# A two-part network on one core: filler matmuls dealt out anew, small tables written by GpSimd, gating tables requested one stage earlier

## The reference

```python
# first model: 16 meta tokens + 256 tokens, width 1024
h = h + 0.5 * swiglu(rms_norm(h, g_ffn1), w1_gate, w1_up, w1_down)
h = h + hybrid_mixer(rms_norm(h, g_mix), ...)      # the attention part, below
h = h + 0.5 * swiglu(rms_norm(h, g_ffn2), w2_gate, w2_up, w2_down)

def hybrid_mixer(u, ...):
    c_q, c_kv, k_pe, fox_qkv, f_logit = split(u @ w_in)
    q = rope(rms_norm(rms_norm(c_q) @ w_uq))           # 8 heads of 96
    k, v = ... rms_norm(c_kv) @ w_ukv ...              # 64 + 32 for keys, 64 for values
    o_mla = causal_attention(q, k, v)
    fq, fk, fv = ... fox_qkv ...                       # 8 more heads of 64
    cum = cumsum(log_sigmoid(f_logit + b_forget))      # adds cum[t] - cum[s] to the scores
    o_fox = causal_attention(rms_norm(fq), rms_norm(fk), fv, cum)
    return concat(o_mla, o_fox) @ w_out

# second model, first layer: the same gated mixer on the latent rows (from the first model)
# and on the 256 context rows (which depend on nothing of the first model)
def gmlp_mixer(h, w_in, b_in, ln_g, ln_b, w_s, b_s, w_out, b_out):
    u, v = split(gelu(h @ w_in + b_in))                # 2048 columns each
    v = layernorm(v, ln_g, ln_b)
    v = einsum('gpq,bcqgd->bcpgd', w_s, v) + b_s.T     # mixes 128 positions
    return (u * v) @ w_out + b_out
# then a routed mixture of experts, a recurrent second layer, a second mixture, a norm
```

## Time and profile before

| | |
|---|---|
| median of 3 runs (lowest, highest) | 3248.51 us (3243.59, 3256.89) |
| the profiled execution's own time / its span | 3252.2 us / 3250.5 us |
| PE busy | 2752.6 us (85% of the span) |
| DVE, ACT, POOL busy | 1076.6 (33%), 521.1 (16%), 319.7 us (10%) |
| mean granted clock of TensorE | 0.938 of full speed |
| the part from the first fox norm to the end of attention | 369.9 to 676 us |
| the latent rows' v stage to the end of `gm_u` | 981.2 to 1107.2 us |

### The profile page before, as it was taken

One profiled execution on the slowest core, in us unless ns is written; L12 is line 12 of the kernel. 1 busy time (PEld: TensorE's weight loads), 2 busy tenths in 40 slices (PEclk: granted clock), 3 DMA queues, 4 the chain that ended last, 5 costly groups with the idle time before them and its releaser, 6 DMA issues. The chain is left out here.

```text
span 3250.5 us, 59101 instructions
## 1 busy us (share of the span) xinstructions
PE 2752.6 (85%) x25857; PEld 1987.0 (61%) x25857; DVE 1076.6 (33%) x2222; ACT 521.1 (16%) x1141; POOL 319.7 (10%) x356
## 2 busy tenths in 40 slices
PE   8999898989998996878777399798989976977775
PEld 7886665668876785444444144388878964444443
DVE  3562326425651413110000421366555522100002
ACT  1001122320001101000000200154444411000001
POOL 1000000000000000201110200132322201111110
PEclk9999989989999997999999699799999987999998
DMA  7684332136865306999999421000000019999994
GB/s 261 236 253 141 106 107 78 40 110 233 256 202 168 104 26 255 338 402 396 405 402 404 137 78 36 19 4 3 4 3 3 4 53 372 403 406 407 407 405 190
DMA packets 297238, 638.61 MB, mean 196 GB/s; under 512 B 29252, under 2 KB 198423, under 8 KB 262436
## 3 DMA queue, kind: packets, MB, share of 16 engines
q1 hardware_dynamic: 254896, 558.44, 46.9%
q10 hardware_dynamic: 30500, 61.96, 5.3%
q0 software_dynamic: 11600, 14.59, 1.4%
HBM read 634.79 MB, written 21.08 MB: 202 GB/s over the span
## 5 line engine op out<-in xcount | busy, mean ns | idle before, releaser
L2426 PE MATMUL bank<-expert_weights,ex_xt 128*64 128x256 f32 x2688 | 314.0, 389 | 90.3 <-DMA expert_weights<-in_moe_w_up_dram 78.0
L2426 PEld LDWEIGHTS bank<-expert_weights,ex_xt 128*64 128x64 f32 x2688 | 216.0, 140 | 202.9 <-issue 133.0
L533 PE MATMUL bank<-u,weights 128*128 128x272 f32 (+1 forms) x1408 | 318.7, 390 | 12.0 <-DVEq L556 12.0
L533 PEld LDWEIGHTS bank<-u,weights 128*128 128x128 f32 x1408 | 270.7, 192 | 59.8 <-DVEq L556 12.6
L1334 DVE SCALAR_TENSOR_TENSOR ada_acc<-ada_w,cond,ada_acc 128x512 f32 (+1 forms) x336 | 227.6, 747 | 1.6 <-PEq L505 1.6
L2337 DVE TENSOR_TENSOR ex_hidden<-ex_silu,bank 128x256 f32<-128x256 f32 x64 | 27.0, 421 | 596.5 <-ACT ex_silu L2475 596.5
L610 PE MATMUL bank<-rw_mixed,weights 128*128 128x512 f32 (+2 forms) x448 | 189.1, 583 | 31.7 <-DVEq L623 28.2
L2426 PE MATMUL bank<-weights,ex_xt 128*64 128x256 f32 x1408 | 168.7, 396 | 38.3 <-DMA weights<-in_moe_w_up_dram 37.0
L2447 PE MATMUL bank<-expert_weights,ex_hidden_turned 128*64 128x512 f32 x672 | 159.3, 617 | 21.7 <-DVE ex_hidden_turned L2340 21.7
L2426 PEld LDWEIGHTS bank<-weights,ex_xt 128*64 128x64 f32 x1408 | 113.5, 143 | 99.9 <-issue 63.5
L610 PEld LDWEIGHTS bank<-rw_mixed,weights 128*128 128x128 f32 (+1 forms) x448 | 84.1, 189 | 137.1 <-issue 135.2
(11 more groups left out here) (593 smaller groups left out, 4264.7 us busy)
## 6 DMA issues: line engine op xcount, KB each, us to landing
expert_weights<-in_moe_w_gate_dram SPq DMA_DIRECT2D x84, 1024.0 KB, 24.3
expert_weights<-in_moe_w_up_dram SPq DMA_DIRECT2D x84, 1024.0 KB, 24.6
expert_weights<-in_moe_w_down_dram SPq DMA_DIRECT2D x84, 1024.0 KB, 24.5
ada_w<-in_ada_w_dram ACTq DMA_DIRECT2D x24, 2048.0 KB, 9.2
weights<-in_moe_w_gate_dram SPq DMA_DIRECT2D x44, 1024.0 KB, 24.2
weights<-in_moe_w_up_dram SPq DMA_DIRECT2D x44, 1024.0 KB, 24.3
weights<-in_moe_w_down_dram SPq DMA_DIRECT2D x44, 1024.0 KB, 24.6
weights<-in_ga_w_in_dram SPq DMA_DIRECT2D x32, 1024.0 KB, 5.6
```

What stands on the lines that cost most here:

```text
L533: last = nc.tensor.matmul(k.bank[b + side * NB][:, 0:N], w[:, f, c * P:(c + 1) * P], rhs[:, f, 0:N], start=(f == 5), stop=(f == 4))
L2426: last = nc.tensor.matmul(half_cols(k.bank[2 + side], t), xt[:, s, f * SLOTS:(f + 1) * SLOTS], w[:, q * 512 + t * 256:q * 512 + t * 256 + ...
```

## The change

- The v pieces are dealt out anew: three units in each of `fqn` and `fkn` (16 pieces behind the loop in place of 8), two in `cq` and `ckv` as before, and six in `expand_stage` in place of eight (none in its last two heads). The banks, the take-over by DVE (`keep_v`, one more in `fqn` and `fkn`, two fewer in `expand`), the GELU shares and SP's requests follow. In `expand_stage` PE issues its first 8 pieces before it waits for `w_uq` and `w_ukv`.
- `mla_sums_of` is written by POOL in `expand_stage`, one stage earlier. The gate tables are preset by POOL in `row_norm_stage`; DVE's two presets in `rope_stage` are gone.
- In attention the u pieces stand behind `scores(u)` and ahead of `turn(u-2)`; they are dealt 2, 1, 1, 2, 1, 1 and, from turn 30 on, 2, 2, 1, 1, 2. ACT takes units over in turns 5, 11, ... 35.
- The four gating tables are requested on ACT at the start of `gmlp_v_stage`, behind the bias; the block that held the requests is gone.

```diff
@@ head_norm_stage (fqn, fkn)
-        block.sync(ahead.feed_v)
+        block.sync(lambda sp: ahead.feed_v(sp, 3))
-            ahead.v_pieces(pe, 2 * DC - 2 * heads)
+            ahead.v_pieces(pe, 3 * DC - 2 * heads)
             ahead.keep_v(dve)
+            ahead.keep_v(dve)
@@ row_norm_stage, pool
-            pool.memset(of[:, :, :], 0.0).then_inc(zeroed, 1)
...
+            for g in gates:
+                pool.memset(g, 1.0).then_inc(preset, 1)
@@ row_norm_stage, tensor
-            pe.wait_ge(marked, HEADS)
@@ expand_stage, tensor
-            k.stream.wait(pe, seg, 0, 0)
-            k.stream.wait(pe, seg, 0, 1)
...
             for h in range(HEADS):
-                ahead.v_pieces(pe, DC)
                 if h < 6:
+                    ahead.v_pieces(pe, DC)
+                    if h == 0:
+                        k.stream.wait(pe, seg, 0, 0)
+                        k.stream.wait(pe, seg, 0, 1)
                     values(h)
@@ expand_stage, pool
+            pool.memset(sums_of[:, :, :], 0.0).then_inc(zeroed, 1)
...
+                pool.memset(sums_of[:, h, h:h + 1], 1.0).then_inc(marked, 1)
@@ rope_stage, vector
-            link(nc.vector.memset(gates_q[0:2, :, :], 1.0))
-            link(nc.vector.memset(gates_k[0:2, :, :], 1.0))
@@ attention_stage, tensor
                     scores(u)
+                ahead.u_pieces(pe, (2, 1, 1, 2, 1, 1)[u % 6] if u < 30 else (2, 2, 1, 1, 2)[u - 30])
...
-                if u < 30:
-                    ahead.u_pieces(pe, (2, 2, 1, 2, 1)[u % 5])
@@ attention_stage, scalar
-                if u % 5 == 0 and 5 <= u <= 30:
+                if u % 6 == 5:
                     ahead.keep_u_scalar(act)
@@ gmlp_v_stage, scalar
             act.dma_start(bias[:, :], ...).then_inc(landed, 16)
+            act.dma_start(tables[0][:, :], k.a["ga_ln_g_2"].to_broadcast([P, GW])).then_inc(tables_landed, 16)
+            act.dma_start(tables[1][:, :], k.a["ga_ln_b_2"].to_broadcast([P, GW])).then_inc(tables_landed, 16)
+            spatial.load(act)
@@ gmlp_norm
-    with nc.Block() as block:
-        @block.scalar
-        def _(act):
-            act.dma_start(g[:, :], k.a["ga_ln_g_2"].to_broadcast([P, GW])).then_inc(landed, 16)
-            act.dma_start(b[:, :], k.a["ga_ln_b_2"].to_broadcast([P, GW])).then_inc(landed, 16)
-            spatial.load(act)
```

More of the change, by code:

```diff
@@ L427, in norm_stage @@
         if ahead is not None:
[L428 removed]
+            block.sync(lambda sp: ahead.feed_v(sp, 2))
         @block.scalar
@@ L828, in _, with row_norm_stage @@
             ahead.keep_v(dve)
-def row_norm_stage(k, name, sides, per, width, ahead):
+            ahead.keep_v(dve)
+def row_norm_stage(k, name, sides, of, gates, width, ahead):
     nc = k.nc
@@ L854, in _ @@
         def _(pool):
-            pool.memset(of[:, :, :], 0.0).then_inc(zeroed, 1)
-            pool.wait_ge(zeroed, 1)
-            for c in range(chunks):
-                for h in range(per):
-                    pool.memset(of[h * step:(h + 1) * step, c, c * per + h:c * per + h + 1], 1.0).then_inc(marked, 1)
+            for g in gates:
+                pool.memset(g, 1.0).then_inc(preset, 1)
         @block.scalar
@@ L889, in _ @@
             ahead.u_pieces(pe, 8)
-            pe.wait_ge(spread, per)
+            pe.wait_ge(spread, 1)
             for n, (src, dst, r, gain, factor, t0, N) in enumerate(sides):
@@ L903, in _ @@
             link = Chain(dve, vdone)
-            for h in range(per):
-                nc.vector.tensor_copy(
-                    to[:, :, h * step:(h + 1) * step],
-                    k.ident[0:HEADS, 0:HEADS].rearrange("r (c h) -> r c h", h=per)[:, :, h:h + 1]
-                    .broadcast_to([HEADS, chunks, step])).then_inc(spread, 1)
+            nc.vector.tensor_copy(to[:, :, :], k.ident[0:HEADS, 0:HEADS].rearrange("r (c h) -> r c h", h=1)
+                                  .broadcast_to([HEADS, HEADS, P])).then_inc(spread, 1)
             def mean(n):
@@ L967, in _ @@
         def _(sp):
-            for _ in range(4):
-                ahead.feed_v(sp)
+            ahead.feed_v(sp, 6)
             sp.wait_ge(made, HEADS * per_head)
@@ L1014, in _ @@
             for h in range(HEADS):
-                ahead.keep_v(dve)
+                if h < 6:
+                    ahead.keep_v(dve)
                 dve.wait_ge(made, 2 * h + 1)
@@ L1024, in _ @@
             ahead.gelu_first(act)
-            for h in range(HEADS):
-                ahead.gelu_unit(act)
-                if h < 6:
-                    (t0, n), half = TT[h % 3], h // 3
-                    act.wait_ge(vmade, h + 1)
-                    nc.scalar.activation(vm[0:n, h % 3, half * 512:half * 512 + 512], k.bank[4 + h % 2][0:n, :], ACT.Copy)\
-                        .then_inc(vemptied, 1)
+            for h in range(6):
+                ahead.gelu_unit(act)
+                (t0, n), half = TT[h % 3], h // 3
+                act.wait_ge(vmade, h + 1)
+                nc.scalar.activation(vm[0:n, h % 3, half * 512:half * 512 + 512], k.bank[4 + h % 2][0:n, :], ACT.Copy)\
+                    .then_inc(vemptied, 1)
+        @block.gpsimd
+        def _(pool):
+            pool.memset(sums_of[:, :, :], 0.0).then_inc(zeroed, 1)
+            pool.wait_ge(zeroed, 1)
+            for h in range(HEADS):
+                pool.memset(sums_of[:, h, h:h + 1], 1.0).then_inc(marked, 1)
+                pool.wait_ge(marked, h + 1)
 def rope_stage(k, q, kk, proj, gates_q, gates_k, ahead):
@@ L1440, in load_spatial_bias, with feed_v @@
             .then_inc(self.bs_landed, 16)
-    def feed_v(self, sp):
-        j = self.v_fed
-        self.v_fed += 1
-        sp.wait_ge(self.v_made, 2 * j + 2)
-        self.k.stream.start_number(sp, self.k.seg["cv"].first + j + RING)
+    def feed_v(self, sp, units):
+        for _ in range(units):
+            self.v_fed += 1
+            if self.v_fed % 2 == 0:
+                sp.wait_ge(self.v_made, self.v_fed)
+                self.k.stream.start_number(sp, self.k.seg["cv"].first + self.v_fed // 2 - 1 + RING)
     def feed_u(self, sp, first, end):
```

49 lines of the change are left out of this document (25 added, 24 removed).

## The result

| | time, us | ratio to before (95% interval) |
|---|---|---|
| before | 3246.05 median (3240.19 to 3256.89, 4 runs) | |
| changed | 3211.71 median (3205.26 to 3226.76, 4 runs) | 0.9893 (0.9865 to 0.9922) |
| changed, later, on another chip | 3209.40 median (3203.76 to 3222.40, 6 runs) | 0.9876 (0.9849 to 0.9904) |

The changed kernel is 34 us faster in the first comparison and 41 us in the later one, 1.1 and 1.2%. The forecast was 3208 us, reached as 44.3 us less than the 3252.2 of the profiled execution of before. The profiled execution of the changed kernel, 3226.76 us, is the slowest of its four. A second profile of the same kernel comes from the later runs (`d1_changed`, span 3205.6 us). The two together help to tell which differences belong to the change and which to an execution.

What follows compares the result with a forecast made beforehand. The prediction took PE to set expand, row norms, attention and the latent v stage, through work issued, clock and gaps. Its terms summed to -44.3 us from 3252.2, giving 3208 us; own range 3198 to 3218, with rivals 3197 to 3238.

Steps and rivals of the forecast that it cites:

- Fillers and the clock behind them: fqn and fkn: two more DVE take-overs cost 0.8 us; shorter PE gaps save 2.9 at half speed, bounds 0 and -5.8.
- Expand: Expand stage: two units of pieces fewer -7.2, wait for w_ukv gone -2.5, half speed behind it -1.7; sum -11.4 us.
- Row norms: Row norms: the table's wait gains 0, the clock falls as before; 0 us, bounds -6.8 and +7.4.
- Rope: Rope: without its two presets DVE starts its 16 turns earlier and paces the stage; -3.7 us, bounds -3.0 and -3.8.
- Attention, stalls: Attention: PE's five waits for ACT's take-over of a u unit go; -2.9 us, bounds 0 and -4.
- Attention, clock: Attention: full clock holds in the middle, half the second slow stretch is saved; -9.0 and -3.0 us, bounds 0 and -15.
- Rival 3: Attention: clock falls in the first turns and stays at half speed to the end; 3281 us, chance 0.07.
- The rule named ahead: Attention: PE's momentary idles between matmul groups swing the clock, so thinner filling could bring falls earlier; no size given.
- Gating tables: Latent v stage to gm_u: idle from ACT's issuing goes -9.7, half speed behind it -2.5; sum -12.2 us.
- Rival 1: Attention: the clock falls about where it did, so its 12.0 us stay; 3220 us, chance 0.25.
- rival 2: Whole kernel: only waits go, clock terms fail or turn, bias late; 3220 us, or 3232 with rival 1; chance 0.15.
- seven stretches at half speed: Stages the change touches: seven stretches at 1.2 GHz, six said to have a PE gap or thin work just ahead.

Runs made afterwards that it cites:

- b2_fill: The kernel before with only the v pieces dealt anew and expand's first 8 pieces ahead of its weight wait; 3239.46 us, ratio 0.9972.
- b4_pool: The kernel before with only POOL writing the sums table in expand and presetting the gate tables in the row norms; 3245.90 us, ratio 0.9993.
- c1_behind: The changed kernel with attention's u pieces behind the mix again, new deal and take-over kept; 3214.79 us, ratio 0.9897 to before.
- b1_tables: The kernel before with only the four gating tables requested on ACT at the start of the latent v stage; 3235.36 us, ratio 0.9960.

## Why the prediction was right, step by step

The time came within 4 us of the forecast, the saving did not: 44.3 us were forecast, 34 and 41 measured. The forecast started from a profiled execution of 3252.2 us, 6 above the median of before in the table, and it counted too much saving in attention; these two errors partly cancel, which is luck.

- **Fillers and the clock behind them, +0.8 and -2.9.** Two take-overs of DVE took 0.74 us at the end of `fqn` (one row, x2). The stretch `fqn` to `ckv` took 41.3 us with 3.4 us at half speed in six of the ten profiles with the new shares and 44.2 with 10.2 in the other four, 42.5 in the mean; the four with the old shares have 43.8. So -1.4 where -2.1 was forecast: the middle between the two bounds is a mixture of both, and not what any one execution does.
- **Expand, -11.4.** Nearly right. The cut from `ckv` to the row norms is 11.47 us shorter in the changed kernel and 11.36 in `b2_fill`, but 0.56 and 0.45 of it are the shorter gap in front of the row norms, so expand itself gave 10.9.
- **Row norms, 0 with bounds -6.8 and +7.4.** Both ends occurred. The table's wait was worth 0.1 us of gap: the first sum now waits for ACT's first square, 0.47 us after ACT starts, in place of the table. In `b4_pool` half speed held until just before the dense run (+7.7 us), as the upper bound has it; in the changed kernel's first profile it held 3.8 us into that run (+9.4 us), which took 6.00 us in place of 4.15. In the second it never came (-6.1; the bound of -6.8 halves the work, where the measured factor of 1.79 gives -6.0). That taking the wait away may itself lengthen the stretch was not in the prediction. This term alone moves the profiled execution above the forecast by more than any other.
- **Rope, -3.7.** Right: 3.66 us. DVE reaches the gate step (L1082) 1.85 us after the stage's start.
- **Attention, stalls, -2.9.** Right for the gaps (7.27 to 4.13 us), about half of it in the stage's length. By the equal turns of the earlier trace rows each us at half speed costs 0.44. With that taken off, attention is 104.2 to 104.7 us long in the four profiles of the old code and 102.7 to 103.4 in the six of the new: 1.5 us less. PE's busy time, reduced in the same way, is 1.1 us higher in the changed kernel's first profile than in that of before; why is open. As to the reason, the named wait went by the deal and the earlier take-over, and the new place of the pieces kept the idle from moving, as `c1_behind` showed.
- **Attention, clock, -9.0 and -3.0.** Right in sign, too large. The term was read from one profile whose attention was slow for its own code: 119.8 us against 117.7 in the mean of four. The new code has 108.1 in the mean of six (105.8 to 110.3). That is -9.5 us with the stalls, where -14.9 was forecast; 18.3 us less at half speed are about -8.1 of it. The late falls went in every profile, as forecast, and the clock is 1.0 in turns 16 to 31. What the term left out are the first turns: the changed kernel's 17.1 us at half speed lie before 570. Rows 2 leave out a stretch of 6.8 us at half speed from 554.9 in the kernel before, across the start of attention, so the sentence that the first turns hold the clock now was wrong. Rival 3 had the place of the falls right, and not that they last.
- The rule named ahead, from the Trainium skill's "TensorE: Matmul & The Clock Gate", section "A second HAM failure mode: psum-queue depth-cycling", is about short idles between groups of matmuls; the prediction took from it that thinner filling could bring the falls earlier. The traces bear it out for the first 40 us of attention (6.2 us at half speed in the mean with the old code, 11.7 with the new, with 1.33 pieces per turn in place of 1.6) and not for the stage: the whole went from 30.0 us (four profiles) to 11.7 (six). Nor is the stretch at 640.6 an example of the section's short idles: PE was busy for all of its 20.40 us.
- **Gating tables, -12.2.** Right: 12.25 us. The four transfers ran at 227 GB/s with the stage's own (149 before) and held up nothing: the bias landed in 4.8 us in place of 4.3, and PE had no wait within the stage. The case in which the bias is requested last was not run.
- **The sum.** In the pair of first profiles, the first expert matmul comes 31.8 us earlier, but the end only 25.5. Of the 6.3 us lost after it, 3.1 are lost between 2589 and 2625 us of before, in the recurrent layer; the rest is spread over several places that I did not follow. In the recurrent layer half-speed stretches of 20.5 and 41.0 us stand in both profiles, with one of 10.2 us ahead of them in the changed kernel and of 3.4 in the kernel before. Windows of 120 and 121 us around them, before and changed:

```profile
2580.00:2700.00 120.00, 91.88 (x1623) 81.70 (x1620) 33.30 (x92) 27.17 (x73) 7.10 (x21) 0.87 0.24 80
```
```profile
2552.00:2673.00 121.00, 92.09 (x1541) 81.74 (x1536) 32.56 (x89) 25.73 (x70) 6.38 (x21) 0.84 0.22 74
```

In the second profile of the changed kernel the part from the first expert to the end takes 3.0 us less than in the first, so about half of the 6.3 is scatter of executions. The rest may be more: the same code took 1945.1 to 1948.5 us in the five profiles of before and of single parts, 1946.6 in the mean, and 1947.5 to 1953.9 in the nine with all parts, 1950.0 in the mean. The single parts ran on another chip than the later kernels, so whether some 3 us are a price of the change is open. Rival 1 (attention's clock as before) and rival 3 (half speed to the end) did not occur; of rival 2 the row norms' part did, in some executions. One count in the prediction is off: of its seven stretches at half speed five stand behind a gap or thin work, as it lists them, and not six.

## What to carry to other kernels

Outside attention, a removed wait or a gap filled with work could be read here from one profile to 0.1 us, and the parts added up. In attention 3.1 us fewer gaps made the stage only 1.5 us shorter, so the stage's length has to be compared too. What the clock costs can't be read from one profile: one stage of the same code or nearly had 0, 3.4, 10.2, 13.7 and 34.1 us at half speed. A term for it should be taken from the mean of several profiles, or compared between profiles in which the clock did the same ahead of the stage, since the slow stretch that one notices in a single profile is likely above its mean. Filler at a stage's start in place of a wait cost nothing here; that it keeps the clock is suggested by one profile and not shown.

## What was not expected of the hardware

POOL's presets of the gate tables, laid "beside 50 us" of the row norms at no cost, slow DVE down. Timeline of POOL and of DVE at the start of that stage in the changed kernel, then DVE in the kernel before:

```profile
458.33 4.29 POOL L856 MEMSET proj<- 2x2176 f32 x2 [38.83 <-POOLq L953]
```
```profile
458.38 2.40 DVE L900 COPY mla_rows_to<-ident 8x1024 f32<-8x1024 f32 x1 [0.68 <-PEq L953]
460.71 0.14 DVE L1506 TENSOR_REDUCE ahead_stats<-ahead_stats 128x2 f32<-128x8 f32 x1
460.88 1.78 DVE L1508 TENSOR_SCALAR ahead_stats<-ahead_stats 128x2 f32<-128x2 f32 x1
```
```profile
474.53 0.68 DVE L905 COPY mla_rows_to<-ident 8x1024 f32<-8x1024 f32 x1 [1.12 <-PEq L960]
475.14 0.14 DVE L1507 TENSOR_REDUCE ahead_stats<-ahead_stats 128x2 f32<-128x10 f32 x1
475.32 0.17 DVE L1509 TENSOR_SCALAR ahead_stats<-ahead_stats 128x2 f32<-128x2 f32 x1
```

The copy takes 2.40 us in place of 0.68 and the tensor_scalar of two columns 1.78 in place of 0.17. POOL's two presets took 1.90 and 2.45 us; the copy ends 0.54 us behind the first, and the tensor_scalar 0.03 us behind the second. The reduce between them keeps its 0.14. The Trainium skill, "SBUF — State Buffer", section "Who interferes with whom", says this: copies and tensor_scalar can take a port pair that DVE shares with GpSimd, one of the two then waits for the other's whole instruction, and tensor_reduce is not touched. The trace agrees in all three. It cost nothing here: without half speed the row norms took 46.39 us with these presets (the second profile) and 46.40 without them (`b1_tables`).
